# Twelve v rows moved from the third mixer stage to the first retrieval lane of a two-layer hybrid encoder

## What is computed

```python
h = layer_norm(ALPHA * h + token_mixers(h, ...))
# peer_ffn, per block of 128 tokens: 8 heads, 16 picks each
q = (xb @ w_q).reshape(128, 8, 2, 128)
s = einsum('thpd,hpnd->thpn', q, sub_keys)         # 2 x 128 keys per head
sv, si = top_k(s, 16)                              # per half
cand = sv[:, :, 0, :, None] + sv[:, :, 1, None, :] # 256 pairs
fs, fi = top_k(cand, 16); experts = the pairs' numbers; g = softmax(fs)
hid = gelu(einsum('td,thkd->thk', xb, u[experts]))
ff  = einsum('thk,thkd->td', g * hid, v[experts])
h = layer_norm(ALPHA * h + ff)
```

## Time and profile before

| what | value |
|---|---|
| time, median of 3 runs | 3570.46 us (3570.24 to 3573.53) |
| profiled execution, its own time | 3578.34 us |
| its span, first to last instruction | 3576.5 us |
| instructions | 32953 |
| read from memory | 1291.65 MB |
| mean granted TensorE clock | 0.932 of full |

### The profile page before, as it was taken

How to read it: one execution, slowest core, us unless ns; L and a number is a source line. 1 busy time by engine, 2 the same in 40 slices (tenths; PEclk the granted TensorE clock), 3 DMA queues, 4 the chain that set the end, 5 groups by cost and what they waited for, 6 DMA issues and landing times.

```text
span 3576.5 us, 32953 instructions
## 1 busy us (share of the span) xinstructions
PE 2935.5 (82%) x10296; PEld 1879.1 (53%) x10296; DVE 2490.6 (70%) x5295; ACT 831.7 (23%) x2384; POOL 1844.3 (52%) x1508
## 2 busy tenths in 40 slices
PE   8999678798789878786689878788689878877776
PEld 6677444366577534355477534357478444432222
DVE  1421577877877877788987877788786887764445
ACT  2310122222210122322210123222220123332222
POOL 0000134686677544578677544578576644545553
PEclk9999799999899989998889989999799999999999
DMA  4334499999899999999999999999999999999997
GB/s 161 112 106 153 156 419 421 397 369 380 322 391 409 409 371 419 421 391 403 395 396 409 409 376 419 414 356 388 337 361 409 409 372 420 418 421 422 421 421 311
DMA packets 281580, 1295.97 MB, mean 362 GB/s; under 512 B 31808, under 2 KB 32064, under 8 KB 211776
## 3 DMA queue, kind: packets, MB, share of 16 engines
q0 software_dynamic: 216576, 1073.84, 74.9%
q1 hardware_dynamic: 64256, 217.94, 16.4%
q10 hardware_dynamic: 576, 2.10, 0.1%
HBM read 1291.65 MB, written 2.10 MB: 362 GB/s over the span
## 4 chain that ended last, share of the span: by engine, by line
PE 23%; DMA 13%; DVE 10%; issue 5%; ACT 2%; POOL 1%; another core or an unknown queue 1%; DVEq 0%; POOLq 0%; ACTq 0%
DMA ring<-in_peer,eidx 11%; PE bank L578 9%; PE bank L820 6%; DVE ring L1189 3%; PE bank L782 2%; DMA work<-in_peer,eidx 2%; DVE acc L1194 2%; PE bank L799 2%; PE bank L653 1%; POOL ring L1151 1%; POOL ring L1156 0%; PE bank L629 0%; DVE work L1189 0%; ACT dg L912 0%
## 5 line engine op out<-in xcount | busy, mean ns | idle before, releaser
L1156 POOL DMA_INDIRECT ring<-in_peer,eidx x808 | 1001.5, 1240 | 408.0 <-issue 232.9
L1189 DVE CUSTOM_DVE_ANT_0 ring<-ring,hp 128x1024 f32<-128x1024 f32 x816 | 983.7, 1222 | 324.7 <-DMA ring<-in_peer,eidx 323.3
L820 PE MATMUL bank<-ring,dg 128*128 128x512 f32 x1784 | 831.1, 615 | 246.6 <-ACT dg L912 238.7
L578 PE MATMUL bank<-xt,panel 128*128 128x256 f32 x4096 | 937.4, 387 | 37.7 <-issue 17.8
L1151 POOL DMA_INDIRECT ring<-in_peer,eidx x390 | 471.9, 1210 | 948.4 <-DVE eidx L1283 427.9
L578 PEld LDWEIGHTS bank<-xt,panel 128*128 128x128 f32 x4096 | 790.6, 194 | 176.0 <-issue 46.8
L820 PEld LDWEIGHTS bank<-ring,dg 128*128 128x128 f32 x1784 | 338.7, 196 | 709.3 <-issue 705.7
L1194 DVE SCALAR_TENSOR_TENSOR acc<-ring,wgt,acc 128x1024 f32<-128x1024 f32 x326 | 416.4, 1288 | 15.5 <-DMA ring<-in_peer,eidx 12.2
L820 PE MATMUL bank<-work,dg 128*128 128x512 f32 x704 | 328.3, 611 | 107.5 <-ACT dg L912 101.1
L1189 DVE CUSTOM_DVE_ANT_0 work<-work,hp 128x1024 f32<-128x1024 f32 x208 | 252.3, 1222 | 123.4 <-DMA work<-in_peer,eidx 120.4
L1151 POOL DMA_INDIRECT work<-in_peer,eidx x154 | 192.8, 1252 | 252.4 <-PE bank L820 100.7
(11 more groups left out here) (174 smaller groups left out, 2464.4 us busy)
## 6 DMA issues: line engine op xcount, KB each, us to landing
panel<-in_panels SPq DMA_DIRECT2D x368, 512.0 KB
ring<-in_peer,eidx POOLq DMA_INDIRECT x1198
work<-in_rel_bias SPq DMA_DIRECT2D x16, 512.0 KB, 8.2
work<-in_peer,eidx POOLq DMA_INDIRECT x306
gb<-in_ln_g SPq DMA_DIRECT2D x8, 512.0 KB
gb<-in_ln_b SPq DMA_DIRECT2D x8, 512.0 KB
panel<-in_keys SPq DMA_DIRECT2D x16, 256.0 KB
work<-in_x SPq DMA_DIRECT2D x4, 512.0 KB, 4.5
```

The source lines that it names most:

```text
L578: ins = mm(dst, w[:, k * P:(k + 1) * P], rhs[:, k, :], start=(k == 0), stop=(k == n - 1))
L820: ins = mm(pa[t * 2 + half][:, :], dg[:, i % DIAGS, :], v_row[:, half * 512:(half + 1) * 512], start=(n == group[0]), stop=(n == group[-1]))
L1156: pool.indirect_dma_start(slots(slot, 1), None, one_row, bass.IndirectOffsetOnAxis(ap=eidx[:, which, t, c:c + 1], axis=0)).then_inc(row_in ...
L1189: v.tensor_tensor_reduce(row, row, hp[:, t, :], 1.0, 0.0, ALU.mult, ALU.add, hid[:, t, c:c + 1]).then_inc(used, 1)
```

## The change

Twelve V rows leave stage C: its units' total goes from 40 to 28. `LAST` goes from 64 to 76, with the number of rows before the lane kept at 16 (`LANE_START`), so the ten slots of T0 hold 56 rows in place of 44. `stream` no longer pairs one V with one U: it spreads the V rows that are not among the last 76 evenly between the U rows (7 V to 8 U), and the counts of U and V in stages B, G and O shift by one or two. In T0 PE takes the V rows with k % 3 != 0, 36 of 56, in place of the odd k, 22 of 44; DVE keeps 20 in place of 22. Over a pass PE sums 40 old V rows in place of 26 and DVE 120 in place of 134. The line numbers of the changed kernel are higher by 3.

```diff
-LAST = 2 * HEAD_ROWS
+LAST = 2 * HEAD_ROWS + 12
+LANE_START = 16
...
-    for head in range(PAIR_HEADS + 2, HEADS):
-        for v, u in zip(v_rows(head - 2), u_rows(head)):
-            rows += [v, u]
-    return rows + v_rows(HEADS - 2) + v_rows(HEADS - 1)
+    us = [row for head in range(PAIR_HEADS + 2, HEADS) for row in u_rows(head)]
+    vs = [row for head in range(PAIR_HEADS, HEADS) for row in v_rows(head)]
+    paced = len(vs) - LAST
+    for i, u in enumerate(us):
+        rows += vs[i * paced // len(us):(i + 1) * paced // len(us)] + [u]
+    return rows + vs[paced:]
...
-MIXER_ROWS = {"A": (16, 60), "B": (10, 22), "C": (12, 40), "R": 6, "G": (10, 64), "O": 16, "N": 4}
+MIXER_ROWS = {"A": (16, 60), "B": (10, 22), "C": (12, 28), "R": 6, "G": (10, 64), "O": 16, "N": 4}
...
-            plan.append(((s, "L", 0, 0), LAST // 4))
-            plan += [((s, "T", 0, i), k) for i, k in enumerate(spread(LAST - LAST // 4 - MIXER_ROWS["N"], CHOICES))]
+            plan.append(((s, "L", 0, 0), LANE_START))
+            plan += [((s, "T", 0, i), k) for i, k in enumerate(spread(LAST - LANE_START - MIXER_ROWS["N"], CHOICES))]
...
-    return kind == "P" or kind == "V" and (stage == "N" or stage == "T" and k % 2 == 1)
+    return kind == "P" or kind == "V" and (stage == "N" or stage == "T" and k % 3 != 0)
```

## The result

The changed kernel takes 3609.85 us (median of 5 runs, 3601.76 to 3614.45), the kernel before 3570.24 us (5 runs, 3566.74 to 3573.53). The ratio is 1.0108, with a 95% interval of 1.009 to 1.0126: the change makes the kernel 39 us slower. The forecast was +36, 3606.4 us, in a range of 3583 to 3622.

The account below looks back on a forecast made before the run. Engines were taken to pace stage C, transfers the stretch from stage G to lane T0's end. Twelve rows into T0 (+46.1), DVE's later last pick (+7.7) and a shorter C (-17.8) gave +36.0 us: 3606.4 us, range 3583 to 3622.

Follow-up runs that it names:

- e1: Kernel before with only PE's share in T0 changed to k % 3 != 0 (28 of 44 rows), no row moved: 3572.9 us, ratio 1.0011.
- e4: Kernel before with the twelve rows of stage C put into stage G, T0 unchanged: 3592.76 us, ratio 1.0072.
- e11: Kernel before with T0's picks 13 and 14 changed over, so DVE's last pick is 13: 3557.53 us, ratio 0.9972.
- e12: Kernel before with T0's pick 14 also given to PE (26 of 44 rows), DVE's last pick 12: 3561.11 us, ratio 0.9981.
- e6: Changed kernel with C at 40 again, odd k on PE, T0 at 32 rows; twelve V rows a pass not computed: 3542.32 us, ratio 0.9886 to before.
- e8: Changed kernel with T0 at 44 rows, odd k on PE; C's twelve V rows a pass not computed: 3567.84 us, ratio 0.9949 to before.
- e10: Kernel before with the last exponential of a stage C unit written ahead of ACT's projection copies: 3583.86 us, ratio 0.9999.
- e13: Kernel before with T0's k = 11 given to DVE and k = 14 to PE, DVE's last pick 12: 3578.42 us, ratio 0.9973.
- e9: Changed kernel with the last exponential of a stage C unit written ahead of ACT's projection copies: 3630.07 us, ratio 1.0104 to before.
- e7: Changed kernel with the move reversed: C at 52, T0 at 32 rows, odd k on PE: 3611.6 us, ratio 1.0072 to before.
- e2: Changed kernel with k % 3 != 2 on PE in T0 (38 of 56 rows), DVE's last pick 14: 3597.74 us, ratio 1.0088 to before.

## What to carry to other kernels

Before moving work, find the stretch in which the transfers never pause and where their pauses are. Work with bytes cost its full transfer time at both places tried in that stretch, whichever engine did it; taken from the stage in front of it, it gives only what that stage's slowest chain gives. When such a stretch ends in a dependency (here new indices), look at which transfer is the last that the dependency waits for, and give those behind it to an engine that nobody waits for: this cost one line and gained 10 us, where every move of rows, either way, lost time. And before moving work the other way, find the floor of the engines' own chain: a stretch gets shorter only down to it, and stalls that were covered stand on the path from there on. An engine that nobody waits for may be late only as long as the buffers that it holds last.

## What the runs showed that I had not expected

- **Chips differ, and in stage G above all.** On the chip on which the kernel before takes 3570 us, the six kernels run there (e1 to e4, e11, e12) have 119.0 us for G in all passes but two of e4's (121.2, 121.9). On the three on which it takes 3582 to 3588, the kernels e6, e8, e10 and e13, with an unchanged G, have 123.7 to 127.4 us in passes 1 and 3, and so has e9 (125.9, 129.1) beside the changed kernel's 119.0. Over G the transfers run at 404 and 405 GB/s all the same (pass 1 of e7 and e10), and PE pauses between matmuls of one panel, as shown under e7. The profile of before that the prediction was made from is of this kind too (124.1, 128.2). Its chip isn't known, and its time is above those of all five timed runs, so it may well be from another chip than they are. In the kernel before T0's wait covers the longer G. What sets it off isn't shown.
- **A late engine is free up to a point, and the point differs by pass.** PE 6 us late behind the new indices costs nothing in passes 1 and 3 and some 4 us in pass 2 (e2, e12); 13 us late in pass 2 (e13) or 19 us in pass 1 (e9) it lowers the transfer share of the following lane from 1.01 to 0.90.
- **A lane that doesn't vary.** Lane T0 took 55.9 to 61.4 us in before, and 44.5 in all six passes of e6 and e7: a time that is the same to a tenth in every pass marks the engine's own chain.
- **One execution can mislead by 16 us.** The two profiles differ by 23 us, the medians by 39; the pieces that the change doesn't touch hold the rest. A and B go with G here: the changed kernel and the six with the short G have 16 to 23 us less in A and B than before's profile, the others between 11 less and 13 more. The two profiles compared are of different kinds.
